# Feed-forwards of 256 tokens: high and low rows side by side in one product of 512 columns

## The reference

```python
D_MODEL = 1024; SEQ = 256; DEPTH = 2
D_FF = D_FF_2 = 2816

def swiglu(h, w_in, w_out):                 # first block
    a, u = jnp.split(h @ w_in, 2, axis=-1)
    return (jax.nn.silu(a) * u) @ w_out

def swiglu_2(h, w_gu, w_down):              # second block
    g, u = jnp.split(h @ w_gu, 2, axis=-1)
    return (jax.nn.silu(g) * u) @ w_down

# first block, each layer l
x = x + g2 * swiglu(h2, w_ffn_in[l], w_ffn_out[l])

# second block, each layer l
x = x + 0.5 * swiglu_2(rmsnorm(x, g_ffn1[l]), w_ffn1_gu[l], w_ffn1_down[l])
x = x + hybrid_mixer(rmsnorm(x, g_mix[l]), ...)
x = x + 0.5 * swiglu_2(rmsnorm(x, g_ffn2[l]), w_ffn2_gu[l], w_ffn2_down[l])
```

## Time and profile before

| | us |
|---|---|
| median of 3 runs | 2602.0 (2597.77 to 2602.44) |
| the profiled execution | 2601.64 |
| its span, first to last instruction | 2599.8 |
| TensorE busy | 2487.0 (96%) |
| TensorE weight loads busy | 2209.9 (85%) |
| VectorE busy | 1422.3 (55%) |
| ScalarE busy | 1147.4 (44%) |
| GpSimd busy | 343.2 (13%) |

### The profile page before, as it was taken

One profiled execution on the slowest core, in us unless ns is written; L12 is line 12 of the kernel. 1 busy time (PEld: TensorE's weight loads), 2 busy tenths in 40 slices (PEclk: granted clock), 3 DMA queues, 4 the chain that ended last, 5 costly groups with the idle time before them and its releaser, 6 DMA issues. The chain is left out here.

```text
span 2599.8 us, 40631 instructions
## 1 busy us (share of the span) xinstructions
PE 2487.0 (96%) x16930; PEld 2209.9 (85%) x16930; DVE 1422.3 (55%) x2367; ACT 1147.4 (44%) x1966; POOL 343.2 (13%) x340
## 2 busy tenths in 40 slices
PE   6998999899999899999999999989999999998998
PEld 3754778788888777899999988989999998898998
DVE  2235335574455445655566566656656566656654
ACT  4243443422222535554454444555445444446443
POOL 1233312000001204300000000230000000023000
PEclk9998999999999899999999999999999999999999
DMA  7523123354454322345565543445555554335544
GB/s 291 210 77 102 63 82 129 111 170 141 152 167 165 122 84 95 130 163 174 173 211 180 177 164 106 132 153 181 177 188 185 165 194 142 126 112 173 181 168 139
DMA packets 70424, 393.45 MB, mean 151 GB/s; under 512 B 6689, under 2 KB 6849, under 8 KB 39905
## 3 DMA queue, kind: packets, MB, share of 16 engines
q1 hardware_dynamic: 60864, 350.93, 39.9%
q0 software_dynamic: 9376, 39.91, 4.4%
HBM read 389.77 MB, written 1.05 MB: 150 GB/s over the span
## 5 line engine op out<-in xcount | busy, mean ns | idle before, releaser
L931 PE MATMUL ps<-h_hi,w_hi 128*128 128x256 f32 (+1 forms) x3424 | 956.7, 311 | 15.3 <-ACT h_hi L1301 13.6
L1658 DVE TENSOR_TENSOR ring_lo<-ring,w_hi 128x1024 fp32r<-128x1024 f32 (+3 forms) x712 | 770.0, 1123 | 338.1 <-ACT w_hi L1253 337.9
L931 PE MATMUL ps<-h_lo,w_hi 128*128 128x256 f32 (+1 forms) x3424 | 942.7, 307 | 0.0
L1253 ACT ACTIVATE w_hi<-ring 128x1024 fp32r<-128x1024 f32 (+3 forms) x712 | 642.8, 951 | 441.8 <-PE ps L931 398.8
L931 PEld LDWEIGHTS ps<-h_hi,w_hi 128*128 128x128 f32 x3424 | 655.5, 192 | 60.3 <-issue 30.7
L931 PEld LDWEIGHTS ps<-h_lo,w_hi 128*128 128x128 f32 x3424 | 655.4, 192 | 28.7
L931 PE MATMUL ps<-h_hi,ring_lo 128*128 128x256 f32 (+1 forms) x3424 | 572.9, 306 | 0.0
L931 PEld LDWEIGHTS ps<-h_hi,ring_lo 128*128 128x128 f32 x3424 | 490.0, 192 | 28.9
L931 PE MATMUL ps<-hid_hi,w_hi 128*128 128x256 f32 (+1 forms) x1056 | 287.9, 301 | 0.0
L931 PE MATMUL ps<-hid_lo,w_hi 128*128 128x256 f32 (+1 forms) x1056 | 287.3, 301 | 0.0
L1583 POOL TENSOR_SCALAR logits<-logits,stat 128x512 f32<-128x512 f32 (+2 forms) x140 | 161.4, 1166 | 618.9 <-DVE stat L1934 618.9
(11 more groups left out here) (245 smaller groups left out, 2339.0 us busy)
## 6 DMA issues: line engine op xcount, KB each, us to landing
ring<-w_ffn_in SPq DMA_DIRECT2D x132, 1024.0 KB, 4.8
ring<-w_ffn_out SPq DMA_DIRECT2D x96, 704.0 KB, 4.1
ring<-w_in SPq DMA_DIRECT2D x42, 1024.0 KB, 4.9
ring<-w_w_in SPq DMA_DIRECT2D x30, 1024.0 KB, 4.9
bias_t<-w_mod POOLq DMA_DIRECT2D x24, 1024.0 KB, 5.4
ring<-w_mod SPq DMA_DIRECT2D x16, 1024.0 KB, 6.3
ring<-w_up SPq DMA_DIRECT2D x16, 576.0 KB, 3.8
ring<-w_pab SPq DMA_DIRECT2D x8, 1024.0 KB, 4.9
```

The lines of the kernel that those rows point to most:

```text
L931: mm = pe.matmul(ps[fs[k].bank][:, 0:n], (hi_w if wpart == "hi" else lo_w)[0:rows, at[k]:at[k] + P], hi if part == "hi" else lo, start=lef ...
L1253: act.activation(w_hi[q.s % 2][:, h * n:(h + 1) * n], ring[q.slot][:, h * n:(h + 1) * n], ACT.Copy)\
L1658: dve.tensor_tensor(ring_lo[q.slot][:, c], ring[q.slot][:, c], plain(w_hi[q.s % 2][:, c]), ALU.subtract)\
```

## The change

In a product of 256 tokens the high and the low rows now lie side by side in SBUF (`h_all`, `hid_all`), 256 columns each. High weights meet both at once, in one matmul of 512 columns, and fill a whole bank: columns 0 to 255 hold the high rows' share and 256 to 511 the low rows'. Low weights meet the high rows in one matmul of 256 columns, into the first half. So three matmuls become two, with the same number of columns. The two halves of the bank must then be added:

- of a gate product VectorE copies 512 columns to SBUF (scaled on the way in the second block, a plain copy in the first), GpSimd adds the halves, and SiLU waits for that;
- of an up product VectorE multiplies 512 columns by the gate, taken twice, GpSimd adds the halves, and the hidden tile's rounding waits for that;
- of an output tile VectorE adds both halves to the residual, one after the other.

VectorE also splits a piece's low halves: the first one stands where both stood, the second follows behind the copy of the gate (`ahead(p, 1)`). Output tiles of 512 tokens, the mixers and layer 0 of the first block keep their three matmuls.

```diff
@@ TensorE, product
+                two = fs[0].two
+                left = [(2 if two else 3) * sum(len(terms) for _, terms in groups)] * len(fs)
...
+                    by_chunk = fresh is not None or need
+                    if two and by_chunk:
+                        order = [(*parts, t, k) for i, t in enumerate(terms)
+                                 for parts in ((("lo", "hi"), ("hi", "both")) if i or left[0] < first else (("hi", "both"), ("lo", "hi")))
+                                 for k in range(len(fs))]
+                    elif two:
+                        order = [("hi", "both", t, 0) for t in terms] + [("lo", "hi", t, 0) for t in terms]
...
+                        mm = pe.matmul(ps[fs[k].bank][:, 0:SQ if part == "both" else n],
+                                       (hi_w if wpart == "hi" else lo_w)[0:rows, at[k]:at[k] + P],
+                                       rows_of[part], start=left[k] == first, stop=left[k] == 1)
@@ ScalarE
-            def hid_part(u, i, T):
-                taken(u)
+            def hid_part(g, i, T):
+                if g["u"].two:
+                    act.wait_ge(halves_summed, g["summed"])
+                else:
+                    taken(g["u"])
...
-                if st["scaled"]:
-                    taken(st["a"])
+                if st["a"].two:
+                    act.wait_ge(halves_summed, st["summed"] - 1)
                     act.activation(t, t, ACT.Silu).then_inc(silu_done, 1)
@@ GpSimd
+            def pool_gate_up(st):
+                i = st["i"]
+                for f, t in ((st["a"], tmp[i % 2]), (st["u"], tmp[2 + i % 2])):
+                    if f.two:
+                        taken(f)
+                        pool.tensor_tensor(t[:, 0:S], t[:, 0:S], t[:, S:SQ], ALU.add).then_inc(halves_summed, 1)
@@ VectorE
-            def ahead(p):
-                while split[0] < p.ahead:
-                    q = splits[split[0]]
+            def ahead(p, keep=0):
+                while split[0] < 2 * p.ahead - keep:
+                    q, h = splits[split[0] // 2], split[0] % 2
...
             def dve_gate_up(st):
-                ahead(st["p"])
                 T, i, a, u = st["T"], st["i"], st["a"], st["u"]
+                ahead(st["p"], 1 if a.two else 0)
...
-                if st["scaled"]:
+                if a.two:
                     full(a)
-                    dve.tensor_tensor(t, ps[a.bank][:, 0:T], row[:, 0:T], ALU.mult).then_inc(psum_taken[a.bank], 1)
+                    if st["scaled"]:
+                        ins = dve.tensor_tensor(by_s(tmp[i % 2], SQ), by_s(ps[a.bank], SQ), on_both(row[:, 0:S]), ALU.mult)
+                    else:
+                        ins = dve.tensor_copy(tmp[i % 2], ps[a.bank][:, 0:SQ])
+                    ins.then_inc(psum_taken[a.bank], 1)
+                    ahead(st["p"])
                     dve.wait_ge(silu_done, st["silu"])
...
+                if u.two:
+                    dve.tensor_tensor(by_s(tmp[2 + i % 2], SQ), on_both(t), by_s(ps[u.bank], SQ), ALU.mult).then_inc(psum_taken[u.bank], 1)
...
                     elif st["how"] == "half":
-                        t = tmp[c % 4][:, 0:S]
-                        dve.tensor_tensor(t, ps[f.bank][:, 0:S], row[:, 0:S], ALU.mult).then_inc(psum_taken[f.bank], 1)
+                        t = tmp[c % 4]
+                        dve.tensor_tensor(by_s(t, SQ), by_s(ps[f.bank], SQ), on_both(row[:, 0:S]), ALU.mult).then_inc(psum_taken[f.bank], 1)
                         taken(f)
-                        dve.scalar_tensor_tensor(xs(c, 0), t, 0.5, xs(c, 0), ALU.mult, ALU.add).then_inc(x_done, 1)
+                        first_half(dve.scalar_tensor_tensor(xs(c, 0), t[:, 0:S], 0.5, xs(c, 0), ALU.mult, ALU.add))
+                        dve.scalar_tensor_tensor(xs(c, 0), t[:, S:SQ], 0.5, xs(c, 0), ALU.mult, ALU.add).then_inc(x_done, 1)
                         continue
```

More of the change, by code:

```diff
@@ L451, in gate_up @@
             u = linear()
+            a.two = u.two = T == S
             if norm:
@@ L454, in gate_up, with resid @@
             add("gate_up", p=p, i=i, T=T, a=a, u=u, fresh=fresh, norm=norm, n=count("hid"), late=i > 0, scaled=scaled,
-                silu=count("silu") if scaled else None, prev=last_u[0])
-            last_u[0] = u
-        def resid(srcs, tiles, T, how, parts, g=None, nxt=None):
+                silu=count("silu") if T == S else None, summed=count("summed", 2) if T == S else None, prev=last_u[0])
+            last_u[0] = plan.items[-1]
+        def resid(srcs, tiles, T, how, parts, g=None, nxt=None, two=False):
             pieces, tiles = [piece(s, n) for s, n in srcs], [(c, linear()) for c in tiles]
+            for _, f in tiles:
+                f.two = two
             xd = [count("x_done") if how == "half" else None for _ in tiles]
@@ L700, in ffn @@
                 resid([(w_out[2 * c + k], 11 * P) for k in range(2)], (c,), S, how,
-                      [[(k // 11, (k % 11) * P, k) for k in range(FT)]], g, nxt)
-                plan.items[-1].update(src=(hid_hi, hid_lo, S, "hid", plan.counts["hid"] - FT))
+                      [[(k // 11, (k % 11) * P, k) for k in range(FT)]], g, nxt, two=True)
+                plan.items[-1].update(src=(lambda lo, k: hid_part_of(lo, k, S), lambda k: both_of(hid_all, k), "hid", plan.counts["hid"] - FT))
         def defer(two=False):
@@ L922, in product @@
                         pe.wait_ge(w_hi_ready, 2 * p.s + 2)
-                    for wpart, part, (at, hi, lo, rows, c), k in order:
+                    for wpart, part, (at, rows_of, rows, c), k in order:
                         if wpart == "lo" and p.n not in lo_seen:
@@ L926, in product @@
                             pe.wait_ge(w_lo_ready, 2 * p.s + 2)
-                        if fresh is not None and wpart == "hi" and k == 0:
-                            pe.wait_ge(h_hi_ready if part == "hi" else h_lo_ready, fresh - KC + c + 1)
-                        if need and part == "hi" and wpart == "hi" and k == 0:
+                        if fresh is not None and k == 0:
+                            if part == "both" or wpart == part:
+                                pe.wait_ge(h_hi_ready, fresh - KC + c + 1)
+                            if part != "hi":
+                                pe.wait_ge(h_lo_ready, fresh - KC + c + 1)
+                            if two and wpart == "lo":
+                                pe.wait_ge(h_hi_ready, fresh - KC + c + 1)
+                        if need and k == 0 and (two or part == wpart):
                             pe.wait_ge(need[0], need[1] + c + 1)
-                        mm = pe.matmul(ps[fs[k].bank][:, 0:n], (hi_w if wpart == "hi" else lo_w)[0:rows, at[k]:at[k] + P],
-                                       hi if part == "hi" else lo, start=left[k] == first, stop=left[k] == 1)
+                        mm = pe.matmul(ps[fs[k].bank][:, 0:SQ if part == "both" else n],
+                                       (hi_w if wpart == "hi" else lo_w)[0:rows, at[k]:at[k] + P],
+                                       rows_of[part], start=left[k] == first, stop=left[k] == 1)
                         left[k] -= 1
@@ L939, in from_h, with rows_of @@
             def from_h(p, at, T, step, stride=None):
[L940 to L941 removed]
+                def rows_of(c):
+                    if stride == SQ:
+                        return dict(hi=at_T(h_hi, c, SQ, 0, T), lo=at_T(h_lo, c, SQ, 0, T))
+                    return dict(hi=h_part(0, c, T), lo=h_part(1, c, T), both=both_of(h_all, c))
+                return [(p, [([c * step + a for a in at], rows_of(c), P, c) for c in range(KC)])]
             def pe_sums(n):
@@ L1635, in _ @@
         def _(dve):
-            chain, split = [0], [0]
+            chain, split, halves = [0], [0], [0]
             def link(ins):
```

92 lines of the change are left out of this document (57 added, 35 removed).

## The result

The changed kernel takes 2625.55 us (median of 4 runs, 2623.19 to 2625.78). The kernel before took 2601.43 in runs on the same chip. The ratio is 1.0095, with a 95% interval of 1.0081 to 1.0108: 24 us slower. The forecast was 2626, slower with a chance of 0.71. The profiled execution's span is 2623.7 us.

The account below looks back on a forecast made before the run. TensorE, 96% busy, bounded the kernel; after the change a 5.77 us chain through VectorE, GpSimd and ScalarE would. 20.0 - 1.1 + 3.2 + 1.3 - 0.8 - 2.0 + 3.7 = +24.3 on 2601.6: 2626 us, range 2612 to 2640 (62%).

Parts of the forecast that it names:

- first up multiplication to first output tile done: Each feed-forward's first output tile ends 4.0 us later: five times, +20.0, less 1.1 for triples before the first gate's scaling.
- output tiles 2 to 8: 7.98 us instead of 7.92 in three feed-forwards, +1.3; first block -0.8; last feed-forward -2.0.
- hand-overs, start and tail: Between stages and at the end: three hand-overs at 0.8, first block to second 0.6, tail 0.7, together +3.7 us.
- The chain of a hidden tile: VectorE, GpSimd and ScalarE steps from one gate's scaling to the next: 5.77 us, above TensorE's new 5.55.
- held to a pitch of 1.56: VectorE's first low half, behind GpSimd's second addition, is held 0.42 us, then takes 1.14.
- TensorE's own pace: Gate and up products: a pair takes 16 x 346.7 ns = 5.55 us; an output tile 7.63 instead of 7.92.
- The stall before the second piece's high halves: In output tiles 2 to 8 ScalarE's high halves come at 4.03, needed at 3.81; TensorE loses some 0.35 us per tile.
- The rescaling: Rescaling of x, eight operations, stands once in VectorE's chain, no longer covered by TensorE's lead: +3.2 us.
- Cheap additions: Rival, 18%: VectorE and GpSimd exclude each other less or the chain has more slack; TensorE stays the bound: 2591 us.
- its term for the starts: In the 2591 us rival, feed-forward starts lose about 0.9 us each, 1.7 more with the rescaling, given as 5.5.
- The lost race: Rival, 7%: VectorE's half starts before GpSimd's second addition in hidden tiles; chain 6.5 us, +79, 2705 us.
- the fixed part: Some 13.3 ns per matmul whatever its width; rival, 5%: it isn't saved, output tiles lose 11.7 us, 2638 us.

Follow-up runs that it names:

- Both halves together: Changed kernel with the second low half moved back to its old place ahead of the gate, beside the first: 2647.4 us, ratio 1.0182 to the kernel before.
- one column: Changed kernel with GpSimd adding 1 column instead of 256, the rest of the sum left out, all waits kept: 2591.2 us, ratio 0.9964 to the kernel before.
- VectorE's additions: Changed kernel with VectorE instead of GpSimd adding the halves of gate and up products: 2596.7 us, ratio 0.9986 to the kernel before.
- behind the up multiplication: Changed kernel with the second low half moved from behind the gate's scaling to after VectorE's multiplication of the up product: 2653.8 us, ratio 1.0205 to before.
- The later input: ScalarE rounds an output tile's second piece before making the next stage's input: 2588.3 us on the kernel where VectorE adds, 2611.0 on the changed kernel.

## Why the prediction was right, step by step

The profiled spans differ by 24.0 us. Three marks that every trace has (first up multiplication, end of the first output tile on TensorE, end of the eighth) divide them; the forecast is sorted the same way, with the 2.0 us that pass between a gate and its up multiplication counted in the hand-overs.

| sum over five feed-forwards | forecast | measured |
|---|---|---|
| first up multiplication to first output tile done, with the rescaling | +13.2 | +9.4 |
| output tiles 2 to 8 | -1.5 | +0.2 |
| hand-overs, start and tail | +12.6 | +14.3 |
| all | +24.3 | +24.0 |

**The chain of a hidden tile** was forecast at 5.77 and measured at 5.735. Its parts: 0.60, addition over at 2.40, SiLU at 2.44 (2.46), low half at 3.84 (3.87), held to a pitch of 1.56 (1.56), then 0.34. The missing 0.035 a tile is 3.7 us over 105 tiles, nearly the whole difference of the table's first line; what is left are terms under 1 us that cancel. Both halves together moved the chain to 5.96, where the sum says 5.98. With one column and with VectorE's additions the sums (4.8 and 4.9) lie under TensorE's pace, and the tiles came at that pace, 5.59; how long the chain itself was there can't be seen from it. Only behind the up multiplication did a sum of this kind fail, by the loop that it left out.

**TensorE's own pace** was forecast at 5.55 for a pair and is 5.59; an output tile takes 7.67, not 7.63. The 226.7 and 120.0 ns hold, but the first five matmuls of 512 columns behind a run of 256 start 228 to 236 ns apart. (All eight of a group take 2.793 us with the eight of 256 behind them, where 8 x 346.7 ns is 2.773.) This was a term mis-sized by 0.04; under the chain it cost nothing in the hidden tiles and 1.4 us in 35 output tiles.

**Output tiles.** The stall before the second piece's high halves was forecast at 0.35 and is 0.38 (8.05 against 7.67), in the first block 0.15 against 0.17. The later input takes it to zero, so the cause was named rightly. The rest of that line is the 0.04 above.

**The rescaling** was forecast at 3.2 and is 3.06 (the first up multiplications are 8.75 apart, and 5.74 in the other feed-forwards of this block). TensorE's stall of 2.90 shows in its row:

```profile
1333.41 1.22 PE L967 MATMUL ps<-h_all,ring_lo 128*128 128x256 f32 x8 [2.90 <-DVE ring_lo L1712]
```

**Hand-overs** were a sum of small terms, forecast 1.7 too low. They can't be read finely: the sums of squares ahead of the first of these feed-forwards start between 1109.1 and 1113.9 us in the ten profiles, though nothing ahead of them differs. That the total agrees to 0.3 us is therefore luck in part; the terms that repeat (5.735, 56.3) are what the argument rests on.

**The rivals.** Cheap additions did not occur, but their price was close: 2591 forecast, 2591.2 once the additions were short (runs from 2589.1 to 2594.7). That it agrees so well is luck in part: its term for the starts is 0.9 five times and 1.7, which is 6.2 and not 5.5, and the short first addition still lasts 1.10. The lost race occurs in the changed kernel only near the end of a feed-forward, behind the tile before the last: there the next low half is a short one (704 columns) and due earlier, the addition behind it lasts 1.4 instead of 0.74, and the next gate comes 5.89 after the last one, although the half is 0.33 shorter. That the fixed part would not be saved is excluded by 5.59 against 5.76.

## What to carry to other kernels

Before work is given to an idle engine, look at what its neighbour does at that moment: GpSimd at 13% was no free helper, since each addition either waited for VectorE's work in SBUF or made it wait, and the same additions on the busier VectorE were faster. Where a saving on the bounding engine is smaller than the slack of the chain behind it, the chain must be summed step by step, with both orders of every race; and an instruction that is moved behind a wait inherits that wait's loop, here TensorE's own.

## What had not been expected of the hardware

After the stall of 2.90 us in the second feed-forward the granted clock fell, and seven distances in a row behind matmuls of 512 columns were 427 ns instead of 227, the lower of the two levels, 1.2 GHz:

```profile
1330.00:1334.00 4.00, 1.10 (x8) 0.68 (x7) 3.33 (x5) 0.02 (x1) 1.64 (x1) 1.00 0.65 256
1334.00:1338.00 4.00, 4.00 (x15) 3.23 (x14) 3.31 (x5) 2.60 (x4) 0.73 (x1) 0.57 0.01 4
```

The columns behind the five engines are the granted clock, the DMA share and GB/s: 1.00, then 0.57. It cost nothing here, because VectorE's chain sets the pace: the up multiplications stay 5.74 apart. Where TensorE sets the pace it does cost: 1.6 us after the stall of 2.17 in the kernel in which VectorE adds. The 0.15 us stalls of the other tiles left the clock at 1.00.
